# A decoder layer on one core: turned keys and outputs of the recurrence made by VectorE in blocks of 32x32

## The reference

```python
h = rms_norm(x, norm_g) * (1 + scale) + shift
qa, ka, va, za, qb, fb, ib, zb = split(h @ w_in)
# branch A: attention in a window of 128 keys, gated by silu(za)
# branch B: a gated linear recurrence, 4 heads of 128, state S (key dim x value dim)
#   o[i]  = (q[i] * decay to i) @ S + sum over j <= i of A[i, j] * v[j]
#   S_new = exp(L_end) * S + sum over j of (k[j] * exp(L_end - L[j]))^T v[j]
yb = rms_norm(o, o_norm_g) * silu(zb)
g_a, g_b = split(sigmoid(h @ w_merge + b_merge))
y = g_a * (ya @ w_proj_a) + g_b * (yb @ w_proj_b)
out = x + gate * (y @ w_out)
```

## Time and profile before

| what | value |
|---|---|
| time, median of 3 runs | 1557.94 us (1557.22 to 1558.79) |
| the profiled execution, span from first to last instruction | 1555.9 us |
| time around the span, against the median | about 2.0 us |
| PE busy | 1527.1 us, 98% |
| DVE busy | 787.0 us, 51% |
| ACT busy | 540.7 us, 35% |
| POOL busy | 826.0 us, 53% |
| instructions | 31655 |

### The profile page before, as it was taken

The page is one execution under the profiler, slowest core; times in us unless marked ns, Lnnn a source line. Parts: engine busy times, 40 slices in busy tenths (PEclk is TensorE's granted clock), DMA queues, the critical chain, the costliest instruction groups (busy, mean ns, idle before and its releaser), DMA issues.

```text
span 1555.9 us, 31655 instructions
## 1 busy us (share of the span) xinstructions
PE 1527.1 (98%) x13048; PEld 1243.0 (80%) x13048; DVE 787.0 (51%) x1900; ACT 540.7 (35%) x1119; POOL 826.0 (53%) x1074
## 2 busy tenths in 40 slices
PE   5999999999999999999999999999999999999998
PEld 2777788877888788888779878888888978888886
DVE  4767464234558866232544774622453775623132
ACT  4334324334322532434331452243432353143330
POOL 0525434557863643365773472437786363437671
PEclk9999999999999999999999999999999999999999
DMA  9612211334453321233343231223544231222351
GB/s 339 243 55 83 83 57 55 111 133 158 168 197 108 110 70 57 82 109 108 137 164 135 92 120 43 83 66 114 208 154 149 75 110 56 78 72 91 102 167 60
DMA packets 62790, 178.94 MB, mean 115 GB/s; under 512 B 7086, under 2 KB 18695, under 8 KB 61864
## 3 DMA queue, kind: packets, MB, share of 16 engines
q1 hardware_dynamic: 62648, 176.93, 33.4%
HBM read 162.84 MB, written 11.96 MB: 112 GB/s over the span
## 4 chain that ended last, share of the span: by engine, by line
PE 95%; DVE 3%; DMA 1%; SPq 1%; issue 1%; ACT 0%; DVEq 0%
PE ps_D L758 56%; PE ps_D L755 25%; PE ps_XCD L820 2%; PE ps_XB L896 1%; PE ps_XB L949 1%; PE ps_XA L954 1%; PE ps_XA L921 1%; PE ps_XA L932 1%; PE ps_XB L948 1%; PE ps_XA L896 1%; DMA th_t<-in_w_ada 1%; SPq L507 1%; PE ps_XB L932 0%; PE ps_XCD L831 0%; PE ps_XCD L939 0%
## 5 line engine op out<-in xcount | busy, mean ns | idle before, releaser
L1702 POOL TENSOR_TENSOR w_lo_t<-w_raw,w_hi_t 128x256 fp32r<-128x256 f32 x920 | 681.0, 775 | 599.7 <-ACT w_hi_t L980 599.4
L758 PE MATMUL ps_D<-h_hi_t,w_hi_t 128*128 128x512 f32 x1024 | 411.2, 402 | 0.0
L758 PE MATMUL ps_D<-h_hi_t,w_lo_t 128*128 128x512 f32 x1024 | 399.6, 390 | 0.0
L758 PE MATMUL ps_D<-h_lo_t,w_hi_t 128*128 128x512 f32 x1024 | 399.5, 390 | 0.0
L980 ACT ACTIVATE w_hi_t<-w_raw 128x1024 fp32r<-128x1024 f32 x232 | 240.0, 1051 | 124.6 <-PE ps_D L755 61.6
L758 PEld LDWEIGHTS ps_D<-h_hi_t,w_hi_t 128*128 128x128 f32 x1024 | 192.3, 188 | 46.3 <-issue 8.9
L758 PEld LDWEIGHTS ps_D<-h_hi_t,w_lo_t 128*128 128x128 f32 x1024 | 192.2, 188 | 41.8
L758 PEld LDWEIGHTS ps_D<-h_lo_t,w_hi_t 128*128 128x128 f32 x1024 | 192.6, 188 | 36.5
L755 PE MATMUL ps_D<-w_hi_t,h_hi_t 128*128 128x384 f32 (+1 forms) x384 | 141.6, 369 | 1.0 <-DVE yf_t L1342 1.0
L755 PE MATMUL ps_D<-w_lo_t,h_hi_t 128*128 128x384 f32 (+1 forms) x384 | 136.6, 356 | 0.0
L755 PE MATMUL ps_D<-w_hi_t,h_lo_t 128*128 128x384 f32 (+1 forms) x384 | 136.3, 355 | 0.0
(11 more groups left out here) (386 smaller groups left out, 2332.9 us busy)
## 6 DMA issues: line engine op xcount, KB each, us to landing
w_raw<-in_w_blocks SPq DMA_DIRECT2D x232, 512.0 KB, 3.4
xr<-in_x_prompt SPq DMA_DIRECT2D x16, 512.0 KB, 5.0
...
```

Of the source, the lines that this page charges most:

```text
L758: ins = mm(bank[:, :], w[:, s0, k0 + k, :], a[:, k, :], start=go, stop=end)
L1702: ins = g_.tensor_tensor(w_lo[:, c, k:k + 2], w_raw[:, n % NRAW, k:k + 2], f32(w_hi[:, c, k:k + 2]), ALU.subtract)
```

## The change

PE no longer turns anything in the recurrence. DVE turns the keys itself: a function `turn` issues 16 transposes for a tile, one for each pair of a source quarter i and a destination quarter j of 32 partitions; each takes 32x32 blocks of all four heads (32 partitions x 128 elements). `KT` t moves to halves 54, 55, 56 and 58, and writes one of four buffers `kst` (named `k_turned` in the rows), which lies where `sza` lay. The copy by ACT is gone. `st` 0 moves from half 57 to half 58; the others stay. The norm is made in two halves of two tiles, at halves 60 and 64. `yD` t (halves 61, 62, 65, 66) turns the normed tile into `yst` (the old `kst` buffer under a new name) and multiplies by the gate from there; `yT` t (halves 65 to 68) is now only the work of ACT and POOL, which wait for it.

```diff
+KT_AT, ON_AT, YD_AT, YT_AT = (54, 55, 56, 58), (60, 64), (61, 62, 65, 66), (65, 66, 67, 68)
...
     for _t in range(NT):
-        put(it, 28 + _t, 0, "KT", _t, "XC")
-        put(it, 28 + _t, 1, "o", _t, "XB")
-        put(it, 28 + _t, 1, "st", _t, "XA")
-    put(it, 32, 0, "onorm", 0)
+        at_half(it, KT_AT[_t], "KT", _t)
+        at_half(it, 57 + 2 * _t, "o", _t, "XB")
+        at_half(it, 57 + 2 * _t + (_t == 0), "st", _t, "XA")
+    for _r in range(2):
+        at_half(it, ON_AT[_r], "onorm", _r)
     for _t in range(NT):
-        at_half(it, 67 + _t, "yT", _t, "XB" if _t % 2 else "XA")
+        at_half(it, YD_AT[_t], "yD", _t)
+        at_half(it, YT_AT[_t], "yT", _t)
...
-                elif task == "KT":
-                    s.wait_ge("lvl", 8 * it + 8)
-                    for h in range(HB):
-                        ins = tr(bank[:, P * h:P * h + P], kk[:, h, P * a:P * a + P], ident[:, :])
...
                 elif task == "st":
-                    s.freed(it, "KT", a)
+                    s.wait_ge("kst", NT * it + a + 1)
                     for h in range(HB):
-                        ins = mm(bank[:, P * h:P * h + P], kst[:, h, :], ibtok[:, a, P * h:P * h + P],
+                        ins = mm(bank[:, P * h:P * h + P], kst[:, a, h, :], ibtok[:, a, P * h:P * h + P],
                                  start=True, stop=True)
-                elif task == "yT":
-                    s.wait_ge("on", 4 * it + a + 1)
-                    for h in range(HB):
-                        ins = tr(bank[:, P * h:P * h + P], kk[:, h, P * a:P * a + P], ident[:, :])
...
+            def turn(dst, t):
+
+                for i in range(0, P, 32):
+                    for j in range(0, P, 32):
+                        s.done(v.transpose(dst[j:j + 32, :, i:i + 32], kk[i:i + 32, :, P * t + j:P * t + j + 32]))
+                s.settle()
...
+                elif task == "KT":
+                    turn(kst[:, a], a)
+                    do(v.memset(idle[:, :], 0.0), "kst")
                 elif task == "onorm":
-                    s.freed(it, "o", 3)
...
+                    s.freed(it, "o", 2 * a + 1)
...
+                elif task == "yD":
+                    turn(yst, a)
+                    do(stt(yf_slot(16 * it + 4 + a), yst[:, :, :], og_half[:, 0:1],
+                           szb[:, :, P * a:P * a + P], ALU.mult, ALU.mult), "yt")
```

More of the change, by code:

```diff
@@ L402, in build @@
         vr = ibtok[:, 0:3, :].rearrange("p j (t c) -> p j t c", c=P)
+        first.close()
+        first = ExitStack()
+        kst = first.enter_context(nc.sbuf_tensor("k_turned", [P, NT, HB, P], F32))
         first.close()
@@ L1124, in side @@
                     s.done(fn(esk, esk, ACT.Exp), "p_exp")
-                elif task == "KT":
-                    s.full(*key)
-                    if it or a:
-                        s.full(*((it, "st", a - 1) if a else (it - 1, "st", 3)))
-                    s.free(fn(kst[:, :, :], bank[:, :].rearrange("p (h n) -> p h n", h=HB), ACT.Copy), *key)
                 elif task == "o":
                     s.full(*key)
+                    s.wait_ge("kst", NT * it + a + 1)
                     if it or a:
@@ L1547, in side @@
                     free(ins, *key)
+                elif task == "KT":
+                    turn(kst[:, a], a)
+                    do(v.memset(idle[:, :], 0.0), "kst")
                 elif task == "onorm":
[L1549 to L1558 removed]
+                    s.freed(it, "o", 2 * a + 1)
+                    c = slice(8 * a, 8 * a + 8)
+                    do(ts(oss[:, c], oss[:, c], 1.0 / P, EPS, ALU.mult, ALU.add))
+                    rsqrt(orst[:, c], oss[:, c], ow1[:, c], ow2[:, c])
+                    for t in (2 * a, 2 * a + 1):
+                        o = kk[:, :, P * t:P * t + P]
+                        s.done(tt(o, o, orst[:, HB * t:HB * t + HB].unsqueeze(2).broadcast_to([P, HB, P]), ALU.mult))
+                    s.settle()
+                elif task == "yD":
+                    turn(yst, a)
+                    do(stt(yf_slot(16 * it + 4 + a), yst[:, :, :], og_half[:, 0:1],
+                           szb[:, :, P * a:P * a + P], ALU.mult, ALU.mult), "yt")
                 elif task == "rstd":
```

21 lines of the change are left out of this document (7 added, 14 removed).

## The result

The changed kernel takes 1632.06 us (1630.03 to 1633.39), the kernel before 1558.36: a ratio of 1.0472, 95% interval 1.0458 to 1.0487. The forecast was 1594 with a range that ended at 1614: the sign and the two waits were right, the loss twice what was forecast. One more execution, the profiled one, took 3028 us with matmuls at twice their usual spacing (0.44 us in place of 0.23); it is in the median of 1632.06 but not in the range and the ratio, and the three others have a median of 1630.73. The rows of the profile after are those of the same kernel, measured and profiled once more.

What follows compares the result with a forecast made beforehand. PE was taken to bound the kernel, busy 98% of the span. Iterations lose 7.1 + 7.1 + 6.0 + 9.7 = 30 us net, the clock 6: 1555.9 + 36 = 1592, plus 2.0 for a median: 1594 us, range 1556 to 1614.

Steps and rivals of the forecast that it cites:

- the price of a PE block: Four transposes on PE in the recurrence: 0.50 us a block, 4.0 an iteration, 16 us for all 32 taken off.
- the turn: 16 DVE transposes per tile, 337 ns apart as copies changing quarters suggest: 5.4 us; products over all partitions suggested 3.7.
- The rivals built on shorter turns: DVE transposes overlap, 226 to 260 ns apart: 1549 to 1555 us, 17%; or turns of 3.1 us or less: 1542, 4%.
- the first wait: PE waits 6.7 us before `o` 1 for DVE's update 0, late behind turns of keys; about 0.6 already at `gb` 0.
- a half has the same small ones and two products, 4.9 us: Each norm half on DVE repeats the old small operations (3.6 us) plus two products; the split adds 3.6 us.
- the second wait: `pa` 0 waits for bank D0, freed by ACT behind `yt` 3: iteration 7.1 us longer, saving and earlier wait included.
- The sum 43.7: DVE's work after update 0 in iteration 3: 5.5 + 3 x 1.2 + 2 x 4.9 + 4 x 6.2 us, `yt` 3 at about 1425.3.
- `yD`'s products slowed by POOL's traffic: Named with a clock lost after each wait for the upper end, 1614 us, of the forecast case (70%).
- DVE goes on without a gap: After update 0, DVE runs its chain to `yD` 3 without idling, since PE and ACT have its inputs by then.
- a state update that waits for PE: Named as a sign of being wrong: DVE's update waiting for PE would mean DVE is not late.
- iteration 0: DVE also has sample rows between `o` 1 and `o` 2 and two column sums, 6.2 us: `pa` 0 9.7 us later.
- the clock: Granted clock falls to 1.2 GHz after PE's gaps: nothing to 4 us an iteration, 1.5 taken, 6 us in all.

Runs made afterwards that it cites:

- whole-width run: Changed kernel with a turn of 4 transposes over all 128 partitions, blocks staying in their own quarter (another result): 1547.78 us, ratio 0.9929.
- the keys alone: Kernel before with only the keys turned by DVE, at the places of the change; norm and outputs as before: 1586.18 us, ratio 1.0179.
- the three runs on it: Changed kernel (1632.06 us); it with a turn's two loops exchanged, so the input's quarter changes (1629.54 us); it with 128-partition transposes staying in their quarter (1547.78 us).
- short-norm run: Changed kernel with the norm's second half left without the 12 small operations of Newton's steps (rougher outputs): 1599.17 us, ratio 1.0265.
- the last version: Against the kernel before: DVE turns keys in pairs and outputs 0 and 1 as a pair, PE outputs 2 and 3; norm whole at its old half: 1551.13 us.
- filler run: Changed kernel with fp32 matmuls that do nothing on PE, seven before `o` 1 and four before `pa` 0: 1626.51 us, ratio 1.0439.

## Why the prediction was wrong

**Right: the price of a PE block.** 0.50 us each, 4.0 an iteration, 16 in all: the whole-width run gives 3.8 to 4.0 for each iteration. The keys' blocks alone gave 0.43 each, so the mean is right and not each place. That it isn't seen in full in a time is due to some 7 us lost behind `pa` 0 in two iterations, by the stalls and the clock after them, which no term held.

**Right: the turn.** 5.31 us with transposes 334 ns apart, forecast 5.4 and 337; `KT` 5.48, forecast 5.5. The choice between the two rows, the copies that change quarters against the products that don't, was the whole question of the sign, and the copies were the right ones: the whole-width form, which doesn't change quarters, lies 203 ns apart. (That the kernel gains with it says nothing on the spacing, since it has 4 transposes a turn instead of 16.) The rule of the Trainium skill that was cited (VectorE: DVE Perf Modes, Two Vector instructions with no wait between them) agrees with the three runs on it: held when the output's quarter or the input's changes, not held in the form that stays, which is also the wider one. The cycle formula of the same page (The TRN2 errata) would make, as an estimate, 0.19 us of the transpose; the unheld spacing is 0.20, so it fits a start-to-start distance without a hold, and neither the held one nor the record of 280 ns. The rivals built on shorter turns fall with this.

**Right: the first wait.** 5.5 or 5.6 us before `o` 1 and 0.6 or 0.7 at `gb` 0 in iterations 1 to 3 (4.3 and 2.6 in iteration 0), forecast 6.7 with 0.6 of it at `gb` 0; the keys alone gave a net loss of 28 us, 7 an iteration.

**Wrong: "a half has the same small ones and two products, 4.9 us", twice, in the second wait.** This is the step that failed. The sum 43.7 has the small operations at the speed they have in the earlier trace rows. Those lie, but for the first, in a stretch where POOL had nothing to do; the second half was moved to one where POOL splits weights and outputs almost without a gap. The earlier trace rows had a sign of it: its first small operation takes 0.65 us where the later ones take 0.17 or 0.18, and it ends as POOL's last instruction does (1397.87). The prediction doesn't use that row:

```profile
1395.05 2.82 POOL L1702 TENSOR_TENSOR w_lo_t<-w_raw,w_hi_t 128x256 fp32r<-128x256 f32 x4 [5.81 <-ACT w_hi_t L980]
1397.93 0.17 DVE L1202 TENSOR_SCALAR sm<-sm 128x16 int32<-128x16 int32 x1
```

Measured, the first half's 15 operations took 3.0 us in iteration 3 and the second's 9.0 in each of iterations 1 to 3 (6.5 in iteration 0). With its products the second half is 10.3 us where 4.9 stood in the sum, 5.4 more; the first half is 4.3, 0.6 less. In iteration 3 the chain from turn 0 to the end of `yt` 3 is 68.5 us against the 62.2 forecast. `pa` 0 then started 69.7 us behind turn 0 (1420.56 to 1490.30), 13.3 later than before instead of 7.1. The text did speak of "`yD`'s products slowed by POOL's traffic": the resource was named, and priced on the wrong instructions. The short-norm run shows that these operations cost 31 us, where 48 at their own 0.2 us would be 10. That the other 21 are contention with POOL follows from the timelines: one operation lasts one of POOL's instructions, in the second half and not in the first, and in the last version, with the norm where POOL is idle, they are short again. No run takes POOL's work away and leaves the place.

The Trainium skill has this (SBUF — State Buffer, Who interferes with whom): an operation of VectorE with two inputs in SBUF, or one in its two-port mode, and one of GpSimd share a port pair, which the first to start holds for its whole instruction, while an operation with at most one input in SBUF outside that mode is free. The trace agrees as far as it goes: small products and scalings lasted one instruction of POOL's each (0.6 to 0.7 or 1.2 us), the turns 5.31 to 5.33 us with POOL beside them or not. Which mode the scalings ran in, no row shows.

**Wrong too: "DVE goes on without a gap".** In iterations 1 to 3 DVE stood idle for PE before update 2 (and once 0.25 us before update 1), 3.1, 2.2 and 1.9 us. The prediction named "a state update that waits for PE" as a sign of being wrong, and it is one. PE came late to `st` 2 mostly because `o` 1, at the lower clock, took 3.4 us (1438.98 to 1442.38), where `o` 2 took 1.8; with the filler matmuls ahead of `o` 1 the gap is 0.5. So the first clock loss wasn't hidden behind DVE's chain: it was in it.

**Wrong: iteration 0.** Forecast 9.7 at the start of `pa` 0, measured 21.8. The chain of DVE, from turn 0 to the end of `yt` 3, explains only 2.0 us of the difference (70.4 against 68.4): 3.5 us of the same contention and 1.0 on a product of the norm are in it, and other terms were shorter than forecast. The other 10.1 are a wait that I didn't look for. In DVE's order `sQ`'s product (L1613), which frees bank XC, stands behind `yD` 3, and the sample's transposes on PE (L837) want XC, ahead of one and a half dense units:

```profile
313.85 1.11 PE L837 MATMUL ps_XCD<-ident,srow 128*128 128x128 f32 x4 [14.03 <-DVE smS L1613]
```

So PE stood for 14.0 us with those units still to do, where in the other iterations it had them behind it, and did them at first at the lower clock: the matmuls of the first 5 us last 0.63 us and start 0.43 apart, against 0.39 and 0.23 at the upper one, 2.2 us lost on eleven of them. I had counted what the sample rows cost DVE, but not who waits for what is queued behind the turns.

**Half right: the clock.** In windows of the changed kernel (length, busy by engine, granted clock):

```profile
1434.00:1438.00 4.00, 0.00 (x0) 0.00 (x0) 3.58 (x14) 1.09 (x2) 2.77 (x4) 0.67 0.00 0
1438.00:1442.00 4.00, 3.02 (x14) 3.05 (x15) 3.68 (x14) 0.00 (x0) 0.00 (x0) 0.50 0.38 131
1442.00:1446.00 4.00, 4.00 (x24) 3.53 (x24) 3.61 (x15) 1.63 (x9) 0.00 (x0) 0.97 0.00 0
```

PE stands still from 1433.4 to 1438.98, and the granted clock is 0.50, that is 1.2 GHz, when it starts again. After the second wait `pa` 0 takes 1.5 us longer than before in iteration 3 (excess 14.9 at its end, 13.3 at its start), 1.8 in iteration 2 and 2.4 in iteration 1: 5.8 us against 1.5 each in the forecast. But to these come the 2.2 us of iteration 0 and the 5.5 us by which DVE's gaps of 7.1 were shorter in the run with filler matmuls: an estimate of some 13 us in all where 6 stood. The filler run itself won 3.3 us net, because it filled one wait, not the other, and added work in iteration 0.

**The sum.** Excess in the four iterations: 21.8 + 15.6 + 15.2 + 14.9 = 67.6 us (rounded from the rows), with the clock after `pa` 0's start in it, against 30 + 6. Behind `pa` 0 6.5 us more are lost (3.1, 1.1 and 2.4 in iterations 0 to 2), and 1.8 are gained ahead of the first turn; that makes the 72.3. Of the 36.3 us missed, 12.1 are iteration 0, 20.1 the longer chain of DVE in iterations 1 to 3 (7.4, 6.4 and 6.3), and 4.7 lie outside the four stretches; 0.6 go off in small terms. The 20.1 are the second half of the norm, 3 x 5.4 = 16.3, and DVE's gaps, 7.1, less 3.3 for terms that were shorter than forecast (the first half of the norm among them). Counted against the first half's speed, the contention itself is 21.3 us in the four iterations (3.5 + 5.9 + 5.9 + 6.0).
